# Weight sums for the block products on GpSimd instead of VectorE, in three feed-forward halves of a two-block transformer kernel

## The reference

```python
def swiglu(x, w13, w2):
    a, b = jnp.split(x @ w13, 2, axis=-1)
    return (jax.nn.silu(a) * b) @ w2

def ffn_half_step(h, g, shift, scale, gate, w13, w2):
    return h + 0.5 * gate * swiglu(modulate(rms_norm_2(h, g), shift, scale), w13, w2)
```

## Time and profile before

| | us |
|---|---|
| median of 3 runs | 3127.92 (3127.85 to 3129.26) |
| time of the profiled execution | 3129.16 |
| its span | 3127.5 |
| TensorE busy | 2982.4 |
| VectorE busy | 2232.3 |
| GpSimd busy | 131.3 |

### The profile page before, as it was taken

The page is one execution under the profiler, slowest core; times in us unless marked ns, Lnnn a source line. Parts: engine busy times, 40 slices in busy tenths (PEclk is TensorE's granted clock), DMA queues, the critical chain, the costliest instruction groups (busy, mean ns, idle before and its releaser), DMA issues. The chain is left out here.

```text
span 3127.5 us, 43825 instructions
## 1 busy us (share of the span) xinstructions
PE 2982.4 (95%) x17228; PEld 2637.7 (84%) x17228; DVE 2232.3 (71%) x3700; ACT 1065.7 (34%) x1640; POOL 131.3 (4%) x99
## 2 busy tenths in 40 slices
PE   8999989999999989889999999999999979999998
PEld 7975567899999867678999998899999857798997
DVE  5667857788887775677888878788887765673434
ACT  4345445233332323134332234333332323332222
POOL 2332310000000000000000000000000000000000
PEclk9998899999999999999999999999999989999999
DMA  5441042333332340242233322333332231443332
GB/s 170 136 149 48 1 128 68 97 113 95 95 102 88 91 138 1 99 115 61 88 99 107 106 88 75 89 94 102 105 111 88 75 94 45 135 139 91 93 94 74
DMA packets 323585, 295.90 MB, mean 95 GB/s; under 512 B 12610, under 2 KB 281028, under 8 KB 321476
## 3 DMA queue, kind: packets, MB, share of 16 engines
q1 hardware_dynamic: 323396, 293.33, 31.6%
HBM read 287.52 MB, written 2.10 MB: 93 GB/s over the span
## 5 line engine op out<-in xcount | busy, mean ns | idle before, releaser
L2697 PE MATMUL PS<-hid_f,w_hi 128*128 128x512 f32 x2112 | 453.2, 336 | 4.8 <-DVE hid_f L2912 4.8
L2697 PEld LDWEIGHTS PS<-hid_f,w_hi 128*128 128x128 f32 x2112 | 323.8, 188 | 48.3 <-DVE hid_f L2912 5.7
L2686 PE MATMUL PS<-x_hi_f,w_hi 128*128 128x384 f32 x912 | 304.7, 334 | 0.0
L2686 PE MATMUL PS<-x_lo_f,w_hi 128*128 128x384 f32 x912 | 304.6, 334 | 0.0
L2686 PE MATMUL PS<-x_hi_f,w_lo 128*128 128x384 f32 x912 | 304.6, 334 | 0.0
L2009 DVE SCALAR_TENSOR_TENSOR ada_product<-ada_w,ada_s 128x1024 f32<-128x1024 f32 x194 | 237.2, 1222 | 49.0 <-DMA ada_w<-in_w_ada_dram 44.6
L2697 PE MATMUL PS<-hid_f,w_lo 128*128 128x512 f32 (+1 forms) x1056 | 269.4, 336 | 0.0
L2778 ACT ACTIVATE w_hi<-w_raw 128x512 fp32r<-128x512 f32 (+1 forms) x315 | 183.6, 604 | 165.4 <-DMA w_raw<-in_w_ffn_dram 118.3
L2686 PE MATMUL PS<-t_hi_f,w_hi 128*128 128x384 f32 x684 | 228.5, 334 | 0.0
L2686 PE MATMUL PS<-t_lo_f,w_hi 128*128 128x384 f32 x684 | 228.5, 334 | 0.0
L2686 PE MATMUL PS<-t_hi_f,w_lo 128*128 128x384 f32 x684 | 228.5, 334 | 0.0
(11 more groups left out here) (434 smaller groups left out, 6578.4 us busy)
## 6 DMA issues: line engine op xcount, KB each, us to landing
w_raw<-in_w_ffn_dram SPq DMA_DIRECT2D x252, 512.0 KB, 5.0
ada_w<-in_w_ada_dram SPq DMA_DIRECT2D x112, 512.0 KB, 3.8
w_raw<-in_w_in_dram SPq DMA_DIRECT2D x46, 512.0 KB, 5.9
w_raw<-in_w_out_dram SPq DMA_DIRECT2D x24, 512.0 KB, 6.8
ada_s<-in_conditions_dram SPq DMA_DIRECT2D x10, 1024.0 KB, 5.2
ada_room<-in_w_ada_dram SPq DMA_DIRECT2D x20, 512.0 KB, 4.0
q_plain<-in_w_ada_dram SPq DMA_DIRECT2D x12, 512.0 KB, 3.9
hT<-hT SPq DMA_DIRECT2D x56, 64.0 KB, 2.0
```

What stands on the lines that cost most here:

```text
L2686: last = nc.tensor.matmul(bank_of(kind), wt[:, k, :], xt[:, k0 + k, :], start=(k == 0 and one == 0), stop=(k == 3 and one == 2))
L2697: last = nc.tensor.matmul(ps[:, a:e], wt[:, f, :], hid[:, f, v, a:e], start=(start and f == 0 and one == 0), stop=(end and f == n - 1 and ...
```

## The change

The four sums of a tile go from VectorE's queue to GpSimd's. GpSimd goes through the same list on its own and makes each sum as soon as its waits allow. `sum_entry(i + 6)` and the two sums ahead of the loop leave VectorE's program. Waits are added: GpSimd waits for the rest of P6 of the tile before; the rest of P5 waits for the sum of P6; the rest of P6 (P7 in tile 3) waits on VectorE for the tile's last sum, that of P3; and SyncE waits for the sum of P3 where it waited for the rest of P4.

```diff
             def wait_made(kind, of):
+                if kind == "P4":
+                    wait_sum(sp, "P3", of)
                 sp.wait_ge(q_ready.sem, b[q_ready] + o.number[at[kind, of]] + 1)
...
-        @block.vector
-        def _(dve):
-            ch = c.dve.on(dve)
+        @block.gpsimd
+        def _(pool):
+            between = c.pool.on(pool)
...
-                wait_raw(dve, o.raw_of(kind, f))
-                wait_quarter(dve, i)
+                wait_raw(pool, o.raw_of(kind, f))
+                wait_quarter(pool, i)
...
                     if f > SEVEN_DIRECT:
-                        wait_sum(dve, "P3", f - 1)
-                    nc.vector.tensor_tensor(out, a21, a22, ALU.add).then_inc(q_sum.sem, 1)
-                    wait_sum(dve, "P5", f)
-                    nc.vector.tensor_tensor(sum_of("P6", f), out, a11, ALU.subtract).then_inc(q_sum.sem, 1)
+                        wait_sum(pool, "P3", f - 1)
+                        pool.wait_ge(q_ready.sem, b[q_ready] + o.number[at["P6", f - 1]] + 1)
+                    nc.gpsimd.tensor_tensor(out, a21, a22, ALU.add).then_inc(q_sum.sem, 1)
+                    wait_sum(pool, "P5", f)
+                    nc.gpsimd.tensor_tensor(sum_of("P6", f), out, a11, ALU.subtract).then_inc(q_sum.sem, 1)
...
                 elif f > SEVEN_DIRECT:
-                    wait_sum(dve, "P6", f)
-                    nc.vector.tensor_tensor(out, a12, sum_of("P6", f), ALU.subtract).then_inc(q_sum.sem, 1)
+                    wait_sum(pool, "P6", f)
+                    nc.gpsimd.tensor_tensor(out, a12, sum_of("P6", f), ALU.subtract).then_inc(q_sum.sem, 1)
+
+            for i in range(len(items)):
+                sum_entry(i)
+
+        @block.vector
+        def _(dve):
+            ch = c.dve.on(dve)
 
             def rest_entry(i):
                 kind, f = o.kind(i)
                 if kind in (None, "R"):
                     return
                 dve.wait_ge(q_hi.sem, b[q_hi] + o.number[i] + 1)
+                if kind == "P5":
+                    wait_sum(dve, "P6", f)
+                elif kind in QUARTER and kind == ("P6" if f > SEVEN_DIRECT else "P7"):
+                    wait_sum(dve, "P3", f)
...
-                sum_entry(i + 6)
                 rest_entry(i + 4)
```

More of the change, by code:

```diff
@@ L225, in start @@
     c.act = Chain(c.tally("act_step"))
+    c.pool = Chain(c.tally("pool_step"))
     c.step = 0
@@ L2871, in sum_entry @@
                     if f == SEVEN_DIRECT:
-                        wait_quarter(dve, at["P6", f])
+                        wait_quarter(pool, at["P6", f])
                     elif f % SEVEN_G == 0:
-                        dve.wait_ge(q_used.sem, b[q_used] + at["R", (f // SEVEN_G - 1, 0)] + 1)
+                        pool.wait_ge(q_used.sem, b[q_used] + at["R", (f // SEVEN_G - 1, 0)] + 1)
                     if f > SEVEN_DIRECT:
-                        wait_sum(dve, "P3", f - 1)
-                    nc.vector.tensor_tensor(out, a21, a22, ALU.add).then_inc(q_sum.sem, 1)
@@ L2880, in sum_entry @@
                 elif kind == "P7":
-                    nc.vector.tensor_tensor(out, a11, a21, ALU.subtract).then_inc(q_sum.sem, 1)
+                    nc.gpsimd.tensor_tensor(out, a11, a21, ALU.subtract).then_inc(q_sum.sem, 1)
                     if f == SEVEN_DIRECT:
-                        wait_quarter(dve, at["P3", f])
+                        wait_quarter(pool, at["P3", f])
                         total_of = sum_of("P3", f)
-                        ch.link(nc.vector.tensor_tensor(total_of, a12, a22, ALU.subtract))
-                        wait_sum(dve, "P7", f)
-                        nc.vector.tensor_tensor(total_of, total_of, out, ALU.add).then_inc(q_sum.sem, 1)
+                        between.link(nc.gpsimd.tensor_tensor(total_of, a12, a22, ALU.subtract))
+                        wait_sum(pool, "P7", f)
+                        nc.gpsimd.tensor_tensor(total_of, total_of, out, ALU.add).then_inc(q_sum.sem, 1)
@@ L2966, in _ @@
             made_direct(1)
-            sum_entry(1)
             rest_entry(0)
@@ L2973, in _ @@
             made_direct(2)
-            sum_entry(4)
             dve.wait_ge(t_rounded.sem, b[t_rounded] + 5)
```

## The result

| | before | after |
|---|---|---|
| median (lowest to highest) | 3127.89 us (3125.97 to 3129.26, 4 runs) | 3309.91 us (3302.88 to 3314.88, 4 runs) |
| ratio, 95% interval | | 1.0581 (1.056 to 1.0601) |
| profiled execution: time, span | 3129.2, 3127.5 us | 3302.88, 3301.1 us |

The change costs 182 us. The forecast was 3321, from 3250 to 3400.

What follows compares the result with a forecast made beforehand. The prediction took the wide halves to be bound by TensorE's stream of matmuls, with VectorE's sums hidden. Its terms, 55 + 83 + 10 + 38 + 7 = 193 us on 3129.2, less 1.2, gave 3321 us, range 3250 to 3400.

Steps and rivals of the forecast that it cites:

- The wait and what is queued behind it: VectorE stops before the rest of P6 for the sum of P3, holding up posts or drains that TensorE's P5 needs.
- T: The moment at which P3 of the tile before is followed by P1 of the next tile on TensorE.
- 39 in-group stalls, 55 us: Tiles following another in their group: P5 at about T+3.5 instead of T+2.08, 1.4 us each, 55 us.
- 15 boundary stalls, 83 us: Where a group begins, drains, a dot and a rest queue behind the blocked rest: 5.5 us each, 83 us.
- the rival: Clock hardly reacts, no collisions, only the two chains: 3266, down to 3230; without the D6 dot 3.1 us per boundary; chance 0.17.
- A second stall at the boundaries, 10 us: Dot of D7 and rest of P7 collide with GpSimd's sums, delaying TensorE's P7: 0.7 us at 14 boundaries, 10 us.
- Clock behind boundaries, 38 us: After 5.5 us idle at a group's start TensorE's clock falls: 2.5 us at each of 15 places, 38 us.
- Clock behind short stalls, 7 us: After the 1.4 us stalls inside groups the clock falls in one of ten: 4 x 1.7, 7 us.
- the first rival: Clock also falls after most short stalls, 66 us instead of 7, and boundaries cost 60 instead of 38: 3402; chance 0.17.
- The start of a half: In tile 3 the last sum is made while direct tile 2 runs; no cost was forecast.
- GpSimd's duration: An undisturbed sum of 128x512 on GpSimd takes 1.28 us, from the profile row; the skill's figure would give 1.12.
- The other sums are lengthened: GpSimd's sums of P5 and P6 take longer than 1.28 us, colliding with VectorE's instructions, which lengthen too.

Runs made afterwards that it cites:

- Run 1: The changed kernel, except that the rest of P3, not the rest of P6, waits for the sum of P3: 3146.46 us, ratio 1.0056.
- run 4: The kernel before, all sums on VectorE, with the sum of P3 made two entries earlier, directly ahead of the rest of P6: 3256.97 us, ratio 1.0408.
- Run 3: The changed kernel with the wait of the rest of P6 for the sum of P3 kept only inside groups and in tile 3: 3207.23 us, ratio 1.0256.
- Run 5: The changed kernel with the dots of D6 moved in the plan to D5: 3268.05 us, ratio 1.0456.
- run 8: Control: the kernel before, all sums on VectorE, with only the dots of D6 moved to D5: 3141.07 us, ratio 1.004.
- run 9: The changed kernel with the wait at the rest of P3, and GpSimd's sum of P3 at each group's first tile after VectorE's rest of P2: 3145.76 us.
- Run 6: The changed kernel with GpSimd making the sum of P3 twice in a row, the second releasing the rest: 3408.26 us, ratio 1.0892.
- Run 7: The changed kernel with the wait moved to the rest of P3 and the dots of D6 moved to D5: 3165.5 us, ratio 1.0122.

## Why the prediction held

- **The wait and what is queued behind it: right.** VectorE stops before the rest of P6, released by the sum of P3, 54 times. The times from T came out as worked out: sum at T+0.30, rest at T+1.69 (1.65 in the forecast), end of L3027 at T+3.44 (3.4), P5 at T+3.54 (3.5), and at the boundary T+7.60 (7.6). Run 1 shows that this place of the wait is the cause, run 4 that no GpSimd is needed for it.
- **39 in-group stalls, 55 us: slightly small.** The profile has 39 x 1.30 of idle time, but the tile's period grows by 1.54, so the term is 60. Run 3 gives 61 above run 1.
- **15 boundary stalls, 83 us: right** (7.60 - 2.08 = 5.5 each). Run 5 takes the dot out of that chain and gets 3.1, the number worked out in the rival, though its dots bring a delay of their own (run 8).
- **A second stall at the boundaries, 10 us: wrong, it is 0.** The list of waits has 54 stalls and no 55th. The step that failed is the time at which the next collisions begin. The forecast put the sums of P5 and P6 at T+9.9, on top of the dot of D7; they start at T+11.8 (728.98), because P5 runs at the slow clock, and by then one dot is done and the other nearly; at all 15 boundaries it is T+11.3 to T+11.9. The rest of P7 did take 1.77 us instead of 0.69 and was done at T+13.7. TensorE came to P7 only at T+15.7 and not at the forecast's T+13.8, held back by the same slow clock. The forecast had both terms, but not that the one takes the ground from the other. Where P5 runs at full clock and the dot comes in its way, as in run 9, the forecast's stall is there, with the dot and the rest of P7 both lengthened, and it is 0.4 to 0.8 us at eight places.
- **Clock behind boundaries, 38 us: the mechanism right, the size a little too large.** It fell at all 15, by 1.3 to 2.9 us each, 2.1 in the mean instead of 2.5, 32 in all.
- **Clock behind short stalls, 7 us: 0.** At 1.30 us the clock holds behind all 39. Run 6 shows that 2.65 us is enough some of the time, so the first rival was wrong for stalls of this length and not in general.
- **The start of a half: put at nothing, it is 3 us.** The forecast let the sums of tile 3 run free beside the direct tiles. They collide with a rest of a direct tile (L191), which takes 3.35 us there instead of 2.29, once in each half, and TensorE waits 3.65 us for it instead of 2.6 to 2.7. VectorE at the start of the first half, then TensorE's waits at all three:

```profile
542.37 3.35 DVE L191 TENSOR_TENSOR w_lo<-w_raw,w_hi 128x2048 fp32r<-128x2048 f32 x1 [0.84 <-ACT w_hi L187]
```

```profile
PE PS L2662 <- DVE w_lo L191: 10.9, 3, 3.7
```

This wait is 10.9 to 11.0 us in every run with the sums on GpSimd and 7.8 to 8.0 in the kernel before and in runs 4 and 8.
- **GpSimd's duration: right.** All 54 sums of P3 took 1.284 to 1.288 us (forecast 1.28), since VectorE stands still beside them. The Trainium skill (GPSIMD Engine Reference, section 3.1) would give 1.12 as an estimate from its row of 2048 elements; the trace has 0.16 more.
- **The other sums are lengthened: right, and so is VectorE.** Groups by shape (number, busy us, mean ns, idle before):

```profile
L2913 DVE TENSOR_TENSOR w_lo<-w_raw,w_hi 128x512 fp32r<-128x512 f32 x291 | 240.1, 825 | 3.2 <-ACT w_hi L2781 1.2 <-issue 0.8
L2913 DVE TENSOR_TENSOR w_lo<-w_plain,w_hi 128x512 fp32r<-128x512 f32 x228 | 200.0, 878 | 250.6 <-POOL w_plain L2894 247.5 <-PE PS L2689 3.1
...
L2883 POOL TENSOR_TENSOR w_plain<-w_plain,w_raw 128x512 f32<-128x512 f32 x57 | 101.2, 1775 | 4.5
...
L2894 POOL TENSOR_TENSOR w_plain<-w_raw,w_plain 128x512 f32<-128x512 f32 x54 | 69.5, 1288 | 213.9 <-issue 211.1 <-PE PS L2689 2.9
```

The rests, of 685 ns before, are at 825 and 878; GpSimd's sum of P6 is at 1775.
- **The total: right, 11 us high.** The terms add up to 193 and the trace has 178: 17 too much in the two terms that are 0, 6 in the clock behind boundaries, 5 too little in the in-group term and 3 in the start of the halves. These errors partly cancel. The median of the runs lies 7 us above the profiled execution, which is part of why the times are nearer to each other than the terms.

## What to carry to other kernels

A wait is paid for by everything that stands behind it in its queue. Before work is given to a free engine, ask which instruction will wait for it, what stands behind that instruction, and when the new producer may start at the earliest. Here the sum was finished far too late for the place of its wait and early enough for its reader. Moving the wait gave back 163 of 182 us; the other 18 stay with the sums on GpSimd, wherever the wait stands. The 163 are not the placement's alone: with VectorE's shorter sum the same placement costs 129 (run 4).

A bound engine isn't helped by taking work from a busy neighbour whose work is already hidden. VectorE lost 158 us of sums and TensorE had never waited for them.

An edit that shifts the order needs a control without the edit it is to help. Run 7 alone (38 us) would have been read as a cost of GpSimd, and 14 of it were the cost of the moved dots.

## What the runs showed of the hardware

- **A longer stall makes a fall of the clock more likely, and there is no sharp edge in these runs.** The granted clock stayed at 1.00 behind all 39 stalls of 1.30 us and behind the eight of 1.1 to 1.8 us in run 1. It fell behind 21 of 39 of 2.65 us (run 6), behind 9 of 15 of 2.9 to 3.7 us (run 5), and behind all 15 of 4.5 us (run 4) and all 15 of 5.4 us (the change). A fall cost 1.3 to 2.9 us of TensorE's time in the change. The length is not all: of eight stalls of 2.94 us in run 5 four were followed by a fall. What else decides isn't known from these runs.
- **Which VectorE instructions GpSimd lengthens.** Those with two SBUF inputs: rests from 0.69 to 1.77, dots from 1.22 to 2.20, in run 1 and in the change. Those with an input in PSUM do not change beside GpSimd's sums: the 57 posts L3022 of run 1, 25 of them beside a sum, took 543 to 558 ns, and the 288 drains L3036 of the change, 34 of them beside one, 468 to 753, against 473 to 753 before. The Trainium skill (SBUF — State Buffer, "Who interferes with whom") says that a VectorE instruction with at most one SBUF input, outside the modes that use two ports, does not contend, and the trace agrees; of its exclusive lock the trace shows the two-input instruction longer by 1.0 to 1.1 us, less than the whole 1.28 of GpSimd's instruction, which had begun up to 0.4 us earlier.
- **The one that begins second pays.** In the changed kernel 62 VectorE instructions with two SBUF inputs were running when a sum began on GpSimd, and none of them is longer by more than 0.01 us. Of the 140 that began while a sum was running, 130 are longer, by up to 1.1 us. GpSimd pays in the same way: its sum takes 1.28 to 1.29 us alone, and 1.40 at 606.88 in run 1, where a dot (605.89, 1.23 us) was still running. The next dot, begun at 607.16 inside that sum, ends 1.08 us behind the sum's end. The two look as if they took turns.
